# Attention in a hybrid decoder layer: normalising the head outputs instead of the probabilities

## The reference

```python
def block(start):
    ...
    logits = (jnp.einsum('bqhd,bqkhd->bhqk', qs, k_sel).astype(jnp.float32) * scale
              + jnp.transpose(bias.astype(jnp.float32), (0, 3, 1, 2)))
    logits = jnp.where(valid[:, None, :, :], logits, -jnp.inf)
    p = jax.nn.softmax(logits, axis=-1).astype(v.dtype)
    out = jnp.einsum('bhqk,bqkhd->bqhd', p, v_sel)
```

## Time and profile before

| | us |
|---|---|
| median of 3 runs | 2406.02 (2402.72 to 2406.24) |
| the profiled execution | 2396.48 |
| its span in the profile | 2394.7 |
| PE busy | 2288.4 (96%) |
| PE weight loads busy | 1928.3 (81%) |
| DVE busy | 1530.2 (64%) |
| ACT busy | 900.5 (38%) |
| POOL busy | 953.8 (40%) |

### The profile page before, as it was taken

How to read it: one execution, slowest core, us unless ns; L and a number is a source line. 1 busy time by engine, 2 the same in 40 slices (tenths; PEclk the granted TensorE clock), 3 DMA queues, 4 the chain that set the end, 5 groups by cost and what they waited for, 6 DMA issues and landing times.

```text
span 2394.7 us, 33923 instructions
## 1 busy us (share of the span) xinstructions
PE 2288.4 (96%) x13028; PEld 1928.3 (81%) x13028; DVE 1530.2 (64%) x1692; ACT 900.5 (38%) x1167; POOL 953.8 (40%) x476
## 2 busy tenths in 40 slices
PE   5999999999988999579999999999999999999998
PEld 1558787887767788579999999999888888888886
DVE  6649874991349564788888888886545333333335
ACT  4334424222336322644444444444322223222222
POOL 6535443543446000245555555554999300000000
PEclk9999999999999999889999999999999999999999
DMA  8977664332232484223333333334776545444443
GB/s 321 356 267 260 235 239 106 97 97 88 81 109 76 151 319 173 86 104 135 133 131 131 131 131 131 131 135 161 263 222 213 162 144 189 145 139 137 144 120 139
DMA packets 129761, 391.22 MB, mean 163 GB/s; under 512 B 18320, under 2 KB 19984, under 8 KB 117520
## 3 DMA queue, kind: packets, MB, share of 16 engines
q1 hardware_dynamic: 115408, 347.65, 42.1%
q10 hardware_dynamic: 9664, 25.70, 2.7%
q0 software_dynamic: 4608, 16.78, 2.4%
HBM read 356.25 MB, written 33.57 MB: 163 GB/s over the span
## 4 chain that ended last, share of the span: by engine, by line
PE 91%; DVE 5%; ACT 1%; issue 1%; DMA 1%; POOL 0%; DVEq 0%; ACTq 0%; SPq 0%; PEldq 0%; POOLq 0%
PE psum L884 29%; PE psum L886 29%; PE psum L885 29%; PE psum L949 1%; PE psum L964 1%; DVE steps L1807 1%; DVE pt_lo L2099 1%; DVE probs L2086 0%; PE psum L926 0%; DVE T_lo L2202 0%; ACT h_raw L1611 0%; DVE B_lo L2202 0%; DVE q_lo L2046 0%; DMA pos_qi<-in_pos_columns 0%; DVE probs L2093 0%
## 5 line engine op out<-in xcount | busy, mean ns | idle before, releaser
L2149 DVE TENSOR_TENSOR w_lo<-raw,w_hi 128x1024 fp32r<-128x1024 f32 x128 | 175.6, 1372 | 424.5 <-ACT w_hi L1573 424.5
L886 PE MATMUL psum<-w_hi,uin_lo 128*128 128x512 f32 x1024 | 406.5, 397 | 0.0
L884 PE MATMUL psum<-w_hi,uin_hi 128*128 128x512 f32 x1024 | 405.9, 396 | 0.0
L885 PE MATMUL psum<-w_lo,uin_hi 128*128 128x512 f32 x1024 | 403.0, 394 | 0.0
L758 POOL TENSOR_TENSOR w_lo<-raw,w_hi 128x1024 fp32r<-128x1024 f32 (+1 forms) x96 | 256.7, 2679 | 337.4 <-ACT w_hi L1307 337.4
L1573 ACT ACTIVATE w_hi<-raw 128x1024 fp32r<-128x1024 f32 x128 | 135.6, 1060 | 491.4 <-PE psum L886 475.8
L884 PE MATMUL psum<-T_hi,w_hi 128*128 128x256 f32 x1024 | 288.9, 282 | 17.1 <-DVE T_lo L2202 17.1
L885 PE MATMUL psum<-T_lo,w_hi 128*128 128x256 f32 x1024 | 288.4, 282 | 0.0
L886 PE MATMUL psum<-T_hi,w_lo 128*128 128x256 f32 x1024 | 288.4, 282 | 0.0
L2143 DVE TENSOR_TENSOR w_lo<-s_tmp,w_hi 128x1024 fp32r<-128x1024 f32 x96 | 222.6, 2320 | 63.7 <-ACT w_hi L1563 63.7
L1307 ACT ACTIVATE w_hi<-raw 128x1024 fp32r<-128x1024 f32 (+1 forms) x128 | 129.0, 1013 | 346.8 <-PE psum L886 312.9
(11 more groups left out here) (307 smaller groups left out, 4712.4 us busy)
## 6 DMA issues: line engine op xcount, KB each, us to landing
raw<-in_w_mlp_down SPq DMA_DIRECT2D x128, 512.0 KB, 3.9
raw<-in_w_in SPq DMA_DIRECT2D x88, 512.0 KB, 3.8
mod_ring<-in_w_mod_first SPq DMA_DIRECT2D x32, 1024.0 KB, 9.0
mod_slab<-in_w_mod SPq DMA_DIRECT2D x32, 1024.0 KB, 5.2
raw<-in_w_up_units SPq DMA_DIRECT2D x64, 512.0 KB, 4.7
unit_odd<-in_w_up_units SPq DMA_DIRECT2D x64, 512.0 KB, 5.0
uin<-u_s SPq DMA_DIRECT2D x128, 256.0 KB, 4.2
raw<-in_w_out SPq DMA_DIRECT2D x32, 512.0 KB, 5.8
```

The lines of the kernel that those rows point to most:

```text
L884: nc.tensor.matmul(o, a_hi, b_hi, start=first, stop=False)
L885: nc.tensor.matmul(o, a_hi, b_lo, start=False, stop=False)
L886: return nc.tensor.matmul(o, a_lo, b_hi, start=False, stop=last)
L2149: V.tensor_tensor(w_lo[:, slot, :, :], raw[:, slot, :, :], w_hi[:, slot, :, :].bitcast(F32), ALU.subtract).then_inc(down_lo, 1)
```

## The change

ACT still computes exp with its row sum, but the probabilities go to the transposes as they are, unnormalised: PE's transposes wait for `exp_ready` in the place of `probs_ready`. The row sums of a whole head are kept (two heads in turn), DVE takes the reciprocal of four columns at once (`head_recip`), and PE transposes each column, broadcast to 128 columns, so that every partition of ROW_BANK holds the row of 512 reciprocals. ACT copies this row to SBUF (`head_row`, in the place of `head_out`), and DVE multiplies the head's output by it on the way out of PSUM (`head_out`, now on DVE). There is one O bank in the place of two, and the first value product of a head waits for the multiply of the head before it. The diff, without the lines that only declare semaphores:

```diff
--- before.py
+++ after.py
@@ -129,10 +129,10 @@
 PROB_SLOTS, BM_SLOTS = 4, 8
 
 S_BANK, SQ_BANK = 4 * (STAGE["out0"] % 2), 4 * ((STAGE["out0"] + 1) % 2)
-O_BANK = SQ_BANK + 1
+O_BANK, ROW_BANK = SQ_BANK + 1, SQ_BANK + 2
 PT_BANK = (S_BANK + 3, SQ_BANK + 3)
 
-LAG_EXP, LAG_NORM, LAG_TURN, LAG_HI, LAG_LO, LAG_PV = 0, 1, 3, 2, 3, 5
+LAG_EXP, LAG_TURN, LAG_HI, LAG_LO, LAG_PV = 0, 3, 2, 3, 5
 TILE_ORDER = ((0,), (1,), (2,), (3,))
 
 
@@ -254,8 +254,8 @@
         pool_fix = sb("pool_fix", [P, CT, 16], F32)
         top8 = sb("top8", [P, 8], F32)
         nmax = sb("nmax", [P, PROB_SLOTS], F32)
-        asum = sb("asum", [P, PROB_SLOTS], F32)
-        arec = sb("arec", [P, PROB_SLOTS], F32)
+        asum = sb("asum", [P, 2 * TT], F32)
+        arec = sb("arec", [P, 2 * TT], F32)
 
 
         def at(kb, name, shape, dt):
@@ -331,6 +331,7 @@
         q_lo = at(116, "q_lo", [P, HEADS, T], F32R)
         k_lo = at(132, "k_lo", [P, HEADS, T], F32R)
         probs = at(60, "probs", [P, PROB_SLOTS, T], F32)
+        arec_row = at(148, "arec_row", [P, T], F32)
         pt_hi = at(68, "pt_hi", [P, 2, TT, 2 * P], F32R)
         pt_lo = at(76, "pt_lo", [P, 2, TT, 2 * P], F32R)
         attn_sq = at(150, "attn_sq", [P, T], F32)
@@ -1106,7 +1108,7 @@
                 if it == 0:
                     pe.wait_ge(act_freed, freed("A", STAGE["g11"] + 1))
                     pe.wait_ge(dve_freed, freed("D", STAGE["g11"] + 1))
-                pe.wait_ge(probs_ready, it + 1)
+                pe.wait_ge(exp_ready, it + 1)
                 if it >= 2:
                     pe.wait_ge(pt_lo_ready, it - 1)
                 for k in range(TT):
@@ -1117,11 +1119,19 @@
             def values_of(pair):
 
                 hd, half = divmod(pair, TT // 2)
-                if half == 0 and hd >= 2:
-                    pe.wait_ge(o_ready, hd - 1)
+                if half == 0 and hd >= 1:
+                    pe.wait_ge(o_ready, hd)
+                if half == 1:
+                    pe.wait_ge(arec_ready, hd + 1)
+                    if hd >= 1:
+                        pe.wait_ge(row_ready, hd)
+                    for k in range(TT):
+                        j = TT * (hd % 2) + k
+                        last = nc.tensor.transpose(psum[:, ROW_BANK, P * k:P * k + P], arec[:, j:j + 1].to_broadcast([P, P]), ident[:])
+                    last.then_inc(row_done, 1)
                 pe.wait_ge(pt_lo_ready, 2 * pair + 2)
                 cols = slice(HD * hd, HD * hd + HD)
-                o = psum[:, O_BANK + hd % 2, 2 * P * half:2 * P * half + 2 * P]
+                o = psum[:, O_BANK, 2 * P * half:2 * P * half + 2 * P]
                 for k in range(TT):
                     last = three(o, v_hi[:, k, cols], v_lo[:, k, cols], pt_hi[:, pair % 2, k, :], pt_lo[:, pair % 2, k, :],
                                  k == 0, k == TT - 1)
@@ -1500,9 +1510,13 @@
 
             def exps(it):
                 act.wait_ge(max_ready, it + 1)
+                hd, t = divmod(it, TT)
+                if t == 0 and hd >= 2:
+                    act.wait_ge(arec_ready, hd - 1)
                 j = it % PROB_SLOTS
+                a = TT * (hd % 2) + t
                 nc.scalar.activation(probs[:, j, :], probs[:, j, :], ACT.Exp, bias=nmax[:, j:j + 1], scale=-1.0,
-                                     accum_out=asum[:, j:j + 1]).then_inc(exp_ready, 1)
+                                     accum_out=asum[:, a:a + 1]).then_inc(exp_ready, 1)
 
             def pt_split(it):
                 act.wait_ge(pt_done, it + 1)
@@ -1512,9 +1526,11 @@
                 nc.scalar.activation(pt_hi[:, pair % 2, :, P * half:P * half + P],
                                      psum[:, PT_BANK[it % 2], :].rearrange("p (k q) -> p k q", k=TT), ACT.Copy).then_inc(pt_hi_ready, 1)
 
-            def head_out(hd):
-                act.wait_ge(pv_done, TT // 2 * (hd + 1))
-                nc.scalar.activation(attn[:, hd, :], psum[:, O_BANK + hd % 2, :], ACT.Copy).then_inc(o_ready, 1)
+            def head_row(hd):
+                act.wait_ge(row_done, hd + 1)
+                if hd >= 1:
+                    act.wait_ge(o_ready, hd)
+                nc.scalar.activation(arec_row[:], psum[:, ROW_BANK, :], ACT.Copy).then_inc(row_ready, 1)
 
             n_it = HEADS * TT
             for it in range(n_it + LAG_PV + 1):
@@ -1527,7 +1543,7 @@
                 if it == TT:
                     s = split_to(s, PROJ_SLABS + RING)
                 if it > LAG_PV and (it - LAG_PV) % TT == 0:
-                    head_out((it - LAG_PV) // TT - 1)
+                    head_row((it - LAG_PV) // TT - 1)
 
 
             act.wait_ge(rinv_ready, 1)
@@ -2086,11 +2102,15 @@
                 V.tensor_tensor_reduce(out=probs[:, j, :], in0=psum[:, S_BANK + it % 3, :], in1=bm[:, it % BM_SLOTS, :], scale=-1.0,
                                        scalar=3e38, op0=ALU.add, op1=ALU.min, accum_out=nmax[:, j:j + 1]).then_inc(max_ready, 1)
 
-            def normalise(it):
-                j = it % PROB_SLOTS
-                dve.wait_ge(exp_ready, it + 1)
-                ch.link(V.reciprocal(arec[:, j:j + 1], asum[:, j:j + 1]))
-                V.tensor_scalar(probs[:, j, :], probs[:, j, :], arec[:, j:j + 1], None, ALU.mult).then_inc(probs_ready, 1)
+            def head_recip(hd):
+                j = TT * (hd % 2)
+                dve.wait_ge(exp_ready, TT * (hd + 1))
+                V.reciprocal(arec[:, j:j + TT], asum[:, j:j + TT]).then_inc(arec_ready, 1)
+
+            def head_out(hd):
+                dve.wait_ge(pv_done, TT // 2 * (hd + 1))
+                dve.wait_ge(row_ready, hd + 1)
+                V.tensor_tensor(attn[:, hd, :], psum[:, O_BANK, :], arec_row[:], ALU.mult).then_inc(o_ready, 1)
 
             def pt_split(it):
                 dve.wait_ge(pt_hi_ready, it + 1)
@@ -2100,11 +2120,13 @@
                                 pt_hi[:, pair % 2, :, q].bitcast(F32), ALU.subtract).then_inc(pt_lo_ready, 1)
 
             n_it = HEADS * TT
-            for it in range(n_it + LAG_LO):
+            for it in range(n_it + LAG_PV + 1):
                 if it < n_it:
                     logits(it)
-                if 0 <= it - LAG_NORM < n_it:
-                    normalise(it - LAG_NORM)
+                if it >= TT and it % TT == 0 and it <= n_it:
+                    head_recip(it // TT - 1)
+                if it >= 2 * TT and it % TT == 1:
+                    head_out(it // TT - 2)
                 if 0 <= it - LAG_LO < n_it:
                     pt_split(it - LAG_LO)
                 if it >= TT and it % TT == 0 and it // TT <= RING:
```

More of the change, by code:

```diff
@@ L449, in build @@
         qk_hi, q_lo_ready, k_lo_ready = sem("qk_hi"), sem("q_lo_ready"), sem("k_lo_ready")
-        s_done, max_ready, exp_ready, probs_ready, pt_done, pt_hi_ready, pt_lo_ready = (
-            sem("s_done"), sem("max_ready"), sem("exp_ready"), sem("probs_ready"), sem("pt_done"),
+        s_done, max_ready, exp_ready, arec_ready, pt_done, pt_hi_ready, pt_lo_ready = (
+            sem("s_done"), sem("max_ready"), sem("exp_ready"), sem("arec_ready"), sem("pt_done"),
             sem("pt_hi_ready"), sem("pt_lo_ready"))
+        row_done, row_ready = sem("row_done"), sem("row_ready")
         pv_done, o_ready, sq_ready, sq_used = sem("pv_done"), sem("o_ready"), sem("sq_ready"), sem("sq_used")
```

## The result

| | before | after |
|---|---|---|
| median, us | 2403.01 (6 runs, 2401.61 to 2406.24) | 2425.05 (6 runs, 2414.64 to 2427.73) |
| profiled execution, us | 2396.48 | 2427.73 |
| its span | 2394.7 | 2425.9 |

The ratio is 1.0084, 95% interval 1.0068 to 1.0101: 16 to 24 us slower, 22.0 by the medians. The forecast had 13.6 us more and 2419.5 us, with a range from 2409 to 2427. It started from a median of 2406.0 for the kernel before; the six runs now give 2403.0.

A forecast was written before the change was run, and what follows sets the result against it. It took PE to bound the kernel overall and DVE the attention stage; start -4.1, five heads +9.1, tail +4.4 and clock +4.2 made +13.6 us over a median of 2406.0, so 2419.5 us, range 2409 to 2427.

The forecast's parts named there:

- Part 1: Attention stage on DVE: 32 normalising steps go, reciprocal and multiply at 0.153 + 0.737 us each on average.
- rival C: Attention stage: the wait for the row does not bind, five heads take 43.2 us against 49.8; -10.3 us, chance 0.09.
- Part 2: Added per head: reciprocal 0.153 us, DVE multiply out of PSUM 0.68, four row transposes 0.35, row copy 0.58.
- Rival E: Attention stage: row transposes cost 0.85 us and the new multiply 1.27; +20.2 us, chance 0.08.
- Part 3: New waits: row lands 2.86 us after the logits step, next value product waits; loop 11.7 us per head.
- the clock: PE gaps of 2.8 us in five heads: 2.5 clock drops expected, 1.7 us each, +4.2 us (0 to 8.5).
- The start: Attention rounds 0 to 9, before the first new multiply: -4.1 us (bounds -6.5 and 0).
- The middle: Five heads, from round 9 to round 29: 58.95 us instead of 49.8, +9.1 us (8.4 to 14.5).
- The tail: From the logits step of round 29 to the output projection: 18.3 us instead of 13.9, +4.4 us (3 to 6).
- Rival B: PE's clock drops after every one of five gaps, 8.5 us in place of 4.2: +17.9 us, 2423.9, chance 0.12.
- A: The wait binds as forecast but PE's clock holds: +9.4 us, 2415.4, chance 0.15.
- D: Nothing to see: queues overlap more and the loop is 1 us shorter; +4.4 us, 2410.4, chance 0.13.

The follow-up runs named there:

- e4: Kernel before, with the reciprocal and normalising multiply left out and nothing put in their place: stage 77.5 us (88.1 before), ratio to before 0.9947.
- e3: Changed kernel with the four row transposes of each head issued twice: stage 112.3 us (109.3 in the changed kernel), ratio to before 1.0089.
- e2: Changed kernel with ten extra matmuls on PE ahead of each head's wait for the multiply: stage 100.1 us, ratio to before 1.0046.
- e1: Changed kernel with ACT's row copy moved to the end of round 4h+8, behind pt_hi: stage 87.6 us, ratio to before 0.9982.
- e5: Changed kernel with ACT's row copy right behind exp of round 4h+8, ahead of pt_hi: stage 81.6 us, ratio to before 0.9972.
- e7: Changed kernel whose multiply, in heads 0 to 6, reads another buffer and doesn't wait for the row: stage 81.6 us, ratio to before 0.9970.
- e8: Kernel before with one O bank in the place of two, nothing else changed: stage 105.8 us, ratio to before 1.0056.
- e6: As e5, with the head's multiply on DVE also moved ahead of the logits step of round 4h+9: stage 81.3 us, ratio to before 0.9964.

## Why the prediction was right

**Part 1, the removed work.** Confirmed by e4: 10.6 us of the stage, five heads in 42.4 us where rival C had 43.2.

**Part 2, the added work.** O measured 0.692 (0.68 forecast), the reciprocal of four columns 0.174 (0.153), R 0.35 to 0.37 for four at the full clock, the row copy 0.593 in the place of 0.586. Rival E falls: e3 prices R at 0.37 to 0.38.

**Part 3, the train and the loop.** Confirmed step by step: row 2.95 after L (2.86), V at 3.80 (3.66), PE idle 3.05 (2.8), in five heads, 2.0 in the next two. The loop without the clock is 12.0 in e2; forecast 11.7, or 12.2 with W. The missing 0.3 to 0.4 is 0.14 in the train, 0.1 in T, which takes 0.44 ahead of R and not 0.35, and 0.1 from the start of the next scores to L, 0.99 and not 0.89 (e2's rows from 761.68 to 769.20). e1, e5 and e7 show that it is the place of the row in ACT's queue alone: the same instructions with the row in an earlier round give 87.6 us at its end (e1) and 81.6 right behind its exp (e5). The single O bank costs at most 1.3 us of the stage when PE hasn't to wait for its release (e7), and 17.7 when it has, even without the rest of the change (e8): it is what hands the wait on to PE. No run has the change with two banks.

**The sum.** The start, forecast at -4.1, came to -3.1: the chain k_hi(2), k_lo(2) and the low clock behind it, which I had as the worse case (L(9) at 17.95 after the first L; it was 18.2). The middle without the clock, +9.1, is +9.7 in e2 (59.6 in the place of 49.8). The tail's +4.4 is +5.3 there.

**The term that was mis-sized is the clock.** I took 2.5 falls of 1.7 us in five gaps, +4.2, and none in the tail. There were four in the five heads, 1.3 to 1.6 us each and 6.0 together (65.5 against 59.6 in e2), and two in the tail, 3.2 together: 109.3 - 100.1 = 9.2 us. Two judgements failed. I counted a 2.74 us gap that was followed by a full clock as evidence of one half for gaps near 3 us; and I set the tail's gaps, at 1.8 to 2.1 by my own working, to nothing, since one of 2.08 had passed. Rival B, a drop after every gap, was nearer than the forecast: it held for six of seven gaps in the changed kernel and six of seven in e3. The Trainium skill (TensorE: Matmul & The Clock Gate, HAM oscillation) describes a kernel whose clock drops in every wait between bursts of matmuls; that a wait of only 2.0 us can be followed by a drop, and that one of 3.06 need not be, is shown by the rows here alone. The sum of the parts with 9.2 in the place of 4.2 is 18.6, inside the measured 16 to 24. Of the 21.1 us in the profile the other 2.5 are +1.0 at the start, +0.6 in the heads and +0.9 in the tail.

**Where luck came in.** The time of 2425.05 us lies in the range and near its upper end. As a difference the range went up to 21 us over 2406.0, and the medians differ by 22.0; that the new median of the kernel before is 3.0 us lower kept the time inside. The mechanism and the direction don't rest on this, the closeness of the number does. The clock's part is also a matter of the execution: the same code had a fall at 368 us in one profile and none in the other.

**The rivals.** A (no clock) is excluded by the windows and by e2's difference. C (faster) named its condition rightly: with the row early, e5 and e6 are faster than before by 6.7 and 8.6 us (0.9972, 0.9964), not by its 10.3. D is excluded by the loop's 12.0. E (R or O dear) is excluded by e3's 0.37 to 0.38 and by O's 0.692.

## What to carry to other kernels

When a step moves to another engine, write down the whole queue ahead of what it waits for, on every engine, and from the round's own start: here five instructions on ACT made a copy of 0.59 us land 2.95 us late, and an earlier place in that queue was worth 21.7 and 27.7 us of the stage (e1, e5). Before a double buffer is given up, look for what it hid: the second O bank hid exactly this train. And price a gap of PE twice, once for its length and once for the lower clock that may follow it.

The version to keep is e5 or e6: the change with the row copied behind exp of round 4h+8 beats both kernels (0.9972 and 0.9964 against 1 and 1.0084), the one before by 0.3 to 0.4%, with intervals that exclude 1.

## What the runs showed of the hardware

A PE gap of 2.02 us was followed by the low level of the clock (0.63 in a window of 4 us), and so was one of 1.97 (0.72), while single gaps of 3.06, 2.08 and, in e3, 2.02 us were not: in these traces the length of one gap doesn't decide. The clock also fell with PE busy throughout (0.53 and 0.61 from 368 to 376), in a stretch that begins with 32 matmuls of one column, where the profile before has 1.00. A fall cost 1.3 to 1.6 us of a chain that PE bounds. Ten matmuls of 512 columns whose result nobody reads, put into such a gap, shortened the stage by 9.2 us in all, with 17.8 us more work on PE.

Transposes of one column broadcast to 128 took 0.35 to 0.37 us for four at the full clock, ordinary ones 0.35.
